# Up projection's last four chunks tile by tile, norm sums split between GpSimd and matmuls, factor diagonal on ScalarE

## What is computed

```python
def rmsnorm(x, g):
    y = x * lax.rsqrt(jnp.mean(x * x, axis=-1, keepdims=True) + EPS) * g
def sqrelu_mlp(h, w1, w2):
    return jnp.square(jax.nn.relu(h @ w1)) @ w2      # w1 (1024, 4096), w2 (4096, 1024)
for i in range(2):
    h = rmsnorm(x, norm_mix[i])
    x = x + (diff_attention(h, ...) if i == 0 else multiscale_pool(h, ...))
    x = x + sqrelu_mlp(rmsnorm(x, norm_mlp[i]), mlp_w1[i], mlp_w2[i])
```

## Time and profile before

| what | us |
|---|---|
| median of 3 runs | 1052.71 (1051.85 to 1053.17) |
| the profiled execution, its own time | 1052.46 |
| span of its trace | 1050.7 |
| PE busy in the span | 989.1 (94%) |
| DVE busy | 874.3 (83%) |
| ACT busy | 479.6 (46%) |
| POOL busy | 429.0 (41%) |

### The profile page before, as it was taken

One profiled execution on the slowest core, in us unless ns is written; L12 is line 12 of the kernel. 1 busy time (PEld: TensorE's weight loads), 2 busy tenths in 40 slices (PEclk: granted clock), 3 DMA queues, 4 the chain that ended last, 5 costly groups with the idle time before them and its releaser, 6 DMA issues.

```text
span 1050.7 us, 12852 instructions
## 1 busy us (share of the span) xinstructions
PE 989.1 (94%) x4676; PEld 802.4 (76%) x4676; DVE 874.3 (83%) x1125; ACT 479.6 (46%) x735; POOL 429.0 (41%) x377
## 2 busy tenths in 40 slices
PE   6999998889899799999999999798999999999998
PEld 5877776667677588887887887696887888788887
DVE  5667889877946999999998897676988989989884
ACT  4525555677644534425435353364452442543420
POOL 5852678556447173473840300371403304124000
PEclk9999999999999999999999999989999999999999
DMA  6423211120232333332333233301323333233102
GB/s 240 146 42 100 61 41 58 63 81 1 62 99 80 100 100 102 99 106 95 108 93 107 74 106 115 120 2 42 119 87 113 100 101 103 98 100 100 61 20 80
DMA packets 52046, 92.74 MB, mean 88 GB/s; under 512 B 8848, under 2 KB 9872, under 8 KB 51984
## 3 DMA queue, kind: packets, MB, share of 16 engines
q1 hardware_dynamic: 45888, 91.24, 27.4%
q10 hardware_dynamic: 6096, 0.69, 0.5%
HBM read 89.82 MB, written 2.10 MB: 87 GB/s over the span
## 4 chain that ended last, share of the span: by engine, by line
PE 53%; DVE 27%; issue 8%; POOL 5%; ACT 4%; DMA 1%; ACTq 1%; DVEq 0%; SPq 0%; POOLq 0%
PE bank L1572 51%; DVE s_s_raw L1342 3%; DVE s_acc L1360 3%; DVE s_lbB_lo L1137 3%; ACT s_u_raw L994 2%; DVE s_w_lo L1117 2%; DVE s_nmax L1227 2%; DVE s_u_raw L1324 2%; POOL s_nsum L727 2%; PE bank L1630 1%; DVE s_u_lo L1348 1%; DVE s_lt_lo L1137 1%; DVE s_p L1249 1%; DVE s_a_lo L1348 1%; POOL s_o_r L702 1%
## 5 line engine op out<-in xcount | busy, mean ns | idle before, releaser
L1572 PE MATMUL bank<-s_hT_hi,s_w_hi 128*128 128x512 f32 x512 | 200.5, 392 | 0.0
L1572 PE MATMUL bank<-s_hT_hi,s_w_lo 128*128 128x512 f32 x512 | 199.4, 389 | 0.0
L1572 PE MATMUL bank<-s_hT_lo,s_w_hi 128*128 128x512 f32 x512 | 199.4, 389 | 0.0
L1117 DVE TENSOR_TENSOR s_w_lo<-s_raw,s_w_hi 128x1024 fp32r<-128x1024 f32 x96 | 165.9, 1744 | 14.3 <-ACT s_w_hi L816 7.9
L1572 PE MATMUL bank<-s_b_hi,s_u_hi 128*128 128x512 f32 x288 | 117.1, 407 | 14.2 <-DVE s_a_lo L1348 10.4
L753 POOL TENSOR_TENSOR s_lt<-s_lbB,s_lbB 128x1024 f32<-128x1024 f32 x14 | 35.0, 2498 | 222.9 <-PE bank L1572 222.9
L846 ACT ACTIVATE s_b_hi<-s_lbB 128x1024 fp32r<-128x1024 f32 x64 | 67.3, 1054 | 128.2 <-POOL s_lbB L753 84.5
L1572 PEld LDWEIGHTS bank<-s_hT_lo,s_w_hi 128*128 128x128 f32 x512 | 96.2, 188 | 20.2 <-issue 0.5
L1572 PEld LDWEIGHTS bank<-s_hT_hi,s_w_hi 128*128 128x128 f32 x512 | 96.2, 188 | 20.2 <-issue 0.5
L1572 PEld LDWEIGHTS bank<-s_hT_hi,s_w_lo 128*128 128x128 f32 x512 | 96.1, 188 | 20.0
L1360 DVE TENSOR_TENSOR s_acc<-s_acc,bank 128x512 f32<-128x512 f32 x168 | 107.5, 677 | 2.0 <-PE bank L1572 2.0
(11 more groups left out here) (195 smaller groups left out, 2186.8 us busy)
## 6 DMA issues: line engine op xcount, KB each, us to landing
s_raw<-in_mlp_w SPq DMA_DIRECT2D x64, 512.0 KB, 3.8
s_lbB<-in_mlp_w SPq DMA_DIRECT2D x64, 512.0 KB, 3.3
s_raw<-in_attn_w_qkv SPq DMA_DIRECT2D x24, 512.0 KB, 4.2
s_raw<-in_attn_w_o SPq DMA_DIRECT2D x8, 512.0 KB, 3.4
s_x_nat<-in_x SPq DMA_DIRECT2D x4, 512.0 KB, 8.5
s_x_again<-in_x SPq DMA_DIRECT2D x4, 512.0 KB, 5.2
out<-s_acc SPq DMA_DIRECT2D x8, 256.0 KB, 2.0
s_raw<-in_pool_w SPq DMA_DIRECT2D x4, 256.0 KB, 2.6
```

The costliest lines, as they stand in the source:

```text
L1117: v.tensor_tensor(w_lo[slot][:, cols], raw[k][:], f32(w_hi[slot][:, cols]), ALU.subtract)\
L1572: return nc.tensor.matmul(o, lhsT, rhs, start=start, stop=stop, **kw)
```

## The change

The up phase takes the chunks 4 to 7 tile by tile instead of only 6 and 7. The sum of squares is divided: POOL adds the squares of chunks 0 to 5, and `stat` adds those of 6 and 7 by matmuls of their own, accumulated in the same place. The squares get four buffers instead of two, and the region moves to the accumulator of P7. In the first blocks `stat` comes after chunk 2. The factor diagonal is made by ACT in four tiles instead of by DVE in one. Orders on ACT and DVE are changed with it. The diff, cut where it only repeats:

```diff
+SUMMED = 6
...
-        nsum, nsq, diag = inside(v_region + P6 * 4 * 1024, ("nsum", [P, S], F32), ("nsq", [P, 2, S], F32),
+        nsum, nsq, diag = inside(v_region + P7 * 4 * 1024, ("nsum", [P, S], F32), ("nsq", [P, 4, S], F32),
...
 def norm_sums(m):                                    # POOL
-                for c in range(NC):
+                for c in range(SUMMED):
...
-                        pool.wait_ge(n_summed, (NC - 1) * m + c - 1)
-                    g.tensor_tensor(nsum[:], first_sum, nsq[:, c % 2, :], ALU.add).then_inc(n_summed, 1)
+                        pool.wait_ge(n_summed, (SUMMED - 1) * m + c - 1)
+                    g.tensor_tensor(nsum[:], first_sum, nsq[:, c % 4, :], ALU.add).then_inc(n_summed, 1)
...
 def w1_hi(b, k):                                     # ACT
-                if k < 3:
-                    act.wait_ge(up_piece, 3 * (b - 1) + k + 1)
+                if k < 2:
+                    act.wait_ge(up_piece, 2 * (b - 1) + k + 1)
                 else:
                     act.wait_ge(h1_ready, CH * b)
...
             def norm_tile(m, c):
+                norm_hi(m, c)
+                norm_square(m, c)
+            def norm_ready(m, c):
                 done, count = ((wo_added, NC), (xt_added, 0), (pool_added, 0))[m]
                 act.wait_ge(done, count + c + 1)
+            def norm_hi(m, c):
+                norm_ready(m, c)
                 a.activation(hT_hi[:, c, :], xT[:, c, :], ACT.Copy, scale=gcol[:, m, c:c + 1]).then_inc(n_hi, 1)
-                if m or c >= 2:
-                    act.wait_ge(n_summed, (NC - 1) * m + (max(1, c - 2) if c >= 2 else 0))
-                a.activation(nsq[:, c % 2, :], xT[:, c, :], ACT.Square).then_inc(n_squared, 1)
+            def norm_square(m, c):
+                norm_ready(m, c)
+                if c >= 4:
+                    act.wait_ge(n_summed, (SUMMED - 1) * m + max(1, c - 4))
+                elif m:
+                    act.wait_ge(n_stat, m)
+                a.activation(nsq[:, c % 4, :], xT[:, c, :], ACT.Square).then_inc(n_squared, 1)
...
+            def norm_diag(layer):
+                act.wait_ge(n_r, 2 * layer + 1)
+                for t in range(NT):
+                    a.activation(diag[:, t * P:(t + 1) * P], ident[:], ACT.Copy, scale=st_r[:, t:t + 1]).then_inc(n_diag, 1)
             def up_phase(b):                         # ACT
-                w2_hi(b, T3)
-                w1_hi(b + 1, 0)
-                w2_hi(b, T2)
-                w1_hi(b + 1, 1)
                 if first(b):
+                    if b:
+                        w2_hi(b, T3)
+                        w2_hi(b, T2)
+                        w1_hi(b + 1, 0)
+                    norm_diag(b // NB)
+                    if b == 0:
+                        w1_hi(b + 1, 0)
+                        w2_hi(b, T3)
+                    w1_hi(b + 1, 1)
                     spread_copy(b // NB)
+                else:
+                    w2_hi(b, T3)
+                    w1_hi(b + 1, 0)
+                    w2_hi(b, T2)
+                    w1_hi(b + 1, 1)
                 square(b, 0)
                 square(b, 1)
                 part_hi(b, A11)
                 part_hi(b, S3)
+                if b == 0:
+                    w2_hi(b, T2)
                 square(b, 2)
                 square(b, 3)
...
-            for c in range(NC):
+            for c in range(4):
                 norm_tile(1, c)
+            for c in range(4, NC):
+                norm_square(1, c)
+            for c in range(4, NC):
+                norm_hi(1, c)
...
             def up_phase(b):                         # DVE; its norm_diag is gone
                 if first(b):
...
                     w2_low(b, B11)
                     if b:
                         w2_low(b, T3)
-                        norm_diag(m)
                         w2_low(b, T1)
+                        w2_low(b, T2)
                         w1_lo(b + 1, 0)
-                        w2_low(b, T2)
                     else:
-                        norm_diag(m)
                         w1_lo(b + 1, 0)
+                        w2_low(b, T3)
                     w1_lo(b + 1, 1)
                     dve.wait_ge(n_rbc, b // NB + 1)
+                    hidden(b, 0)
                 else:
...
                     w2_low(b, T2)
+                    hidden(b, 0)
                     w1_lo(b + 1, 1)
-                hidden(b, 0)
                 hidden(b, 1)
                 part_sum(b, S3)
                 part_lo(b, A11)
-                hidden(b, 2)
-                if b == 0:
-                    w2_low(b, T3)
-                hidden(b, 3)
-                part_lo(b, S3)
                 if b == 0:
                     w2_low(b, T1)
+                hidden(b, 2)
+                part_lo(b, S3)
+                hidden(b, 3)
+                if b == 0:
                     w2_low(b, T2)
...
             for c in range(4, NC):
                 add_turned(c)
-                if c > 4:
-                    norm_lo(1, c - 1)
-            norm_lo(1, NC - 1)
+            for c in range(4, NC):
+                norm_lo(1, c)
...
             def up_last(b, f):                       # PE
-                if f == 0:
-                    pe.wait_ge(w_lo_done, 4 * w1_slab(b) + 4)
-                up_part(b, f, NC - 2)
-                up_part(b, f, NC - 1).then_inc(h1_ready, 1)
+                for c in range(4, NC):
+                    if f == 0 and c % 2 == 0:
+                        pe.wait_ge(w_lo_done, 4 * w1_slab(b) + c // 2 + 1)
+                    last = up_part(b, f, c)
+                last.then_inc(h1_ready, 1)
             def up(b):
-                for k in range(3):
+                for k in range(2):
...
             def stat(m):
-                pe.wait_ge(n_summed, (NC - 1) * (m + 1))
+                pe.wait_ge(n_squared, NC * (m + 1))
+                pe.wait_ge(n_summed, (SUMMED - 1) * (m + 1))
                 for t in range(NT):
-                    last = mm(bank[(7 + 4 * ((m + 1) // 2)) % 8][:, t:t + 1], nsum[:, t * P:(t + 1) * P], ones[:, 0:1], start=True, stop=True)
+                    dst, cols = bank[(7 + 4 * ((m + 1) // 2)) % 8][:, t:t + 1], slice(t * P, (t + 1) * P)
+                    mm(dst, nsum[:, cols], ones[:, 0:1], start=True)
+                    for c in range(SUMMED, NC):
+                        last = mm(dst, nsq[:, c % 4, cols], ones[:, 0:1], stop=c == NC - 1)
                 last.then_inc(n_stat, 1)
             def spread(n):
-                pe.wait_ge(n_diag, n + 1)
+                pe.wait_ge(n_diag, NT * (n + 1))
...
-            first_tiles(0, range(5))
+            first_tiles(0, range(3))
             stat(0)
-            first_tiles(0, (5,))
+            first_tiles(0, (3,))
             first_last(0)
...
-            first_tiles(NB, range(2, 6))
+            first_tiles(NB, (2,))
             stat(2)
+            first_tiles(NB, (3,))
             first_last(NB)
```

More of the change, by code:

```diff
@@ L1314, in norm_v @@
                     .then_inc(n_v, 1)
-            def norm_diag(m):
-                dve.wait_ge(n_r, m + 1)
-                v.tensor_tensor(diag[:].rearrange("p (t q) -> p t q", t=NT),
-                                ident[:].unsqueeze(1).to_broadcast([P, NT, P]),
-                                st_r[:, 0:NT].unsqueeze(2).to_broadcast([P, NT, P]), ALU.mult).then_inc(n_diag, 1)
             def hidden(b, f):
@@ L1365, in up_phase @@
                 if first(b):
-                    m = 2 * (b // NB)
-                    norm_v(m)
+                    norm_v(2 * (b // NB))
                     w2_low(b, B11)
@@ L1799, in first_last @@
             def first_last(b):
-                m = 2 * (b // NB)
-                pe.wait_ge(n_lo, NC * m + NC)
+                pe.wait_ge(n_lo, NC * 2 * (b // NB) + NC)
                 up_last(b, 0)
```

## The result

| us | before | after |
|---|---|---|
| median of 4 runs each | 1052.94 (1051.85 to 1059.13) | 1038.18 (1036.47 to 1039.57) |
| the profiled execution, span | 1052.46, 1050.7 | 1036.47, 1034.7 |

The ratio is 0.9847, 95% interval 0.9805 to 0.9889: 1.5% faster. The changed kernel, measured once more on another chip beside the kernel before, gave 1039.03 against 1052.71, ratio 0.9865 (0.9843 to 0.9887). The forecast of 1032.7 was 5.5 us too low; its range holds the result.

What follows compares the result with a forecast made beforehand. PE, busy 94% of the span, was taken to bound the kernel. Gains of 5.8, 5.2 and 9.0 made 20.0 us: 1052.46 to 1032.5, plus 0.25 for the median, 1032.7; range 1025.5 to 1040 for 8 in 10.

Steps and rivals of the forecast that it cites:

- the rival of the clock: The clock falls in the longer `stat`, in the first blocks and the pooling chain: 5 us lost, 1037.7; chance 0.2.
- that of the pooling: Pooling's gain is given back at DVE's locked low part and the additions behind: 4 to 6 us less, 1038; chance 0.1.
- the signs that I had named for being wrong: DVE ahead of PE at the end of up, `stat(0)` starting much after 324, or low clock following `stat`.
- Part 1: Chunks 4 to 7 tile by tile, hidden 0 earlier: A11's wait goes over 12 blocks, 5.8 us, bounds 4 and 9.7.
- The stop at the last product: At an ordinary block's last product, 0.39 us lost, expected to stay because POOL starts before DVE's low part of A22.
- the first rival: DVE starts before POOL at block end: last-product stop goes in some 10 blocks, 3.9 us more, 1028.8; chance 0.15.
- Hidden 0's place: In ordinary blocks, hidden 0 goes ahead of the last w1 split on DVE, so low A11 comes with over 1 us spare.
- Plain blocks: Blocks 7 and 15 were costed at nothing: DVE reaches hidden 0 late, or PE has turns of x between.
- Block 0: Products' 13th matmul starts at 345.8 against 351.02: 5.2 us gained, 1.2 of it low clock; bounds 3.7 and 6.7.
- `stat` (2.4 us): 24 matmuls instead of 8, 2.4 us instead of 0.80, adding 1.6 us of PE work in each of three places.
- Pooling and block 8: An earlier sum of squares and earlier windows, then block 8 without its stop: 9.0 us gained together, bounds 6 and 10.5.
- My bound for the lock: In the pooling, DVE's low part held behind POOL's last difference may move the 4.5 us gain between 3.2 and 5.8.

Runs made afterwards that it cites:

- experiment 6: Changed kernel with DVE taking low A22 before the P6 gathers and the P5 gathers before T4's low part; 1037.42 us, ratio 0.9812.
- experiment 8: Changed kernel with hidden 0 of ordinary blocks put back behind the last w1 split; 1036.27 us, ratio 0.982.
- experiment 7: Changed kernel with POOL's fourth difference of block 8 moved behind the norm's root; 1038.05 us, ratio 0.9833.
- the second execution: The profiled execution of the unedited changed kernel's repeated measurement on another chip; that measurement gave 1039.03 us, ratio 0.9865.
- experiment 10: Changed kernel with `stat` between chunk 3's matmuls in block 8 alone, and low A22 and P5 gathers moved earlier on DVE; 1033.88 us, ratio 0.9822.
- experiment 3: Changed kernel with `stat` placed between the matmuls of chunk 3 in blocks 0 and 8; 1036.86 us, ratio 0.983.
- experiment 9: Changed kernel with `stat` placed between the matmuls of chunk 3 in block 8 alone; 1037.13 us, ratio 0.9856.

## Why the prediction was right, and where it was off

*Faster, and the range:* right. The median lies at the rival of the clock (1037.7, chance 0.2) and at that of the pooling (1038, chance 0.1), not within the forecast's own 1029.5 to 1036. Of the signs that I had named for being wrong one came: the low clock follows `stat`. That the range holds the result is in part luck, since 2.0 us found elsewhere made up for some of what was missing: without them the median would be 1040.2, just outside.

*Part 1 (5.8 us):* right: the stop at the end of up is gone in all 14 blocks, 2.7 and 3.0 us over the two layers' ordinary blocks, alone 6.8 with the plain block. The stop at the last product stayed, as reckoned, for the reason given (experiment 6). My margin of 0.25 us in the first rival was real: in the changed kernel DVE comes 0.30 us behind POOL's start in block 9 (770.44, 770.14), and one gather of 0.6 us put behind the low part makes it 0.30 ahead (experiment 6). Hidden 0's place, of which I made a step, does nothing (experiment 8).

*Plain blocks (0):* wrong by 1.0 us. In block 7 the distance of starts ahead of the first down product fell from 1.34 to 0.36 us. In block 15 it stayed at 1.46.

*Block 0 (5.2 us):* the size is right, 5.8 and 4.2, its makeup isn't, so the size is luck. The matmul at 351.02, from which I reckoned, is the tenth of the products; the 13th starts at 351.70, so that my own steps give 5.9. Sum, diagonal and spread went as forecast: the 13th starts 29.69 us after the block, against 33.93. That is 4.2, less than 5.9 by 1.7, of which the low clock behind `stat` is 1.6. The other 1.5 came behind it, where I had S2's low part late by about 1 us again: with PE slower ahead of it that stop is gone, with full clock it is back with 0.69 (experiment 7), because DVE's splits behind POOL's differences are the next bound.

*`stat` (2.4 us):* 24 records took 2.6 to 2.7, 0.111 each, at full clock. The term was sized well. What I put apart as a rival, that the clock falls behind or in it, happened in five of the eight profiled executions that kept this row of 24 in block 0, 7 to 12 matmuls each time; behind `stat(2)` it cost 1.6, in four of the six that kept the row there, against my "up to 1.5 us in each first block".

*Pooling and block 8 (9.0 us):* this is the step that failed. Up to `stat(1)` it gave its 3.9. Behind it I had 5.1 more and got nothing. Three parts of it:
- "PE, which ran the pooling map in between at the low clock and now has the full one, starts the windows at 684.1", 6.4 us after `stat(1)`. It hasn't. PE stood 1.1 us ahead of `stat(1)`, and in all nine executions with that stop the clock still fell, 1.0 to 3.9 us after the row's start, in the row or in the map behind it; the windows start 7.0 to 8.8 us after `stat(1)`, against 6.93 before. I took the low clock of the map for a result of the stop of 5.3 us, and the stop's end for the clock's return. 0.5 to 2.3 us in the two executions. In the first, where DVE's fourth low part ends 6.7 us after the row's start, DVE's chain has a share in it.
- "From here the gain may shrink or grow by one lock": it shrank, from 1.86 to 2.60 us of the held low part, the stop grew from 0.69 to 1.44, and the clock fell behind it. Windows 2.5 to 3.6 us longer. My bound for the lock, 1.3 us, left the clock out. This is the largest part.
- The rest, 4.5 forecast from the last window to the end of block 8, was 4.1 where the clock held behind `stat(2)` and 2.5 where it didn't.

Of the 5.5 us between forecast and median, 3.4 is this sum (5.2 and 0.2 missing, 1.3, 0.6 and 0.1 found elsewhere), 0.5 is the stage ahead of block 0, and 1.5 that the profiled execution lay 1.7 below its median, where I had added 0.25. Where the clock falls explains a part of that: the second execution lost 2.8 us more in the same stages.

What stays open: what in the state of PE decides in which execution the clock falls behind the row; no run here controls it. That DVE's chain can hold up the squares of block 8 was seen in experiment 7 alone. Why the clock fell behind the stops of 0.91 us and more in the windows, and not behind those of 0.69 and less, is open too: no run set the length of that stop but experiment 7, which took it away. The 1.56 us of block 4 in experiment 6 came again with experiment 10 (that block 42.70 us); its cause, POOL's preparation of the band matrices beside DVE in that block alone, is read from the trace and wasn't tried.

## What to carry to other kernels

A short stop of PE is priced by what the clock does behind it as well, and a row of one-column matmuls in PE's stream can bring the same, even with PE busy by every row. Between wide matmuls they brought no fall in four places of experiments 3, 9 and 10, against nine falls behind the 14 rows of 24 that stood in the first blocks of the changed kernel and of those made from it; but where something waits for their sum this costs more than the fall (block 0 of experiment 3). Where two engines share a lock, the order on the one decides which of them waits, and a move that makes PE faster changes who comes first: look at each place where they meet, block by block. And compare stages by their length in the trace, not by the total, when a stage that isn't touched varies by more than the edit.

## What the runs showed that I had not expected

- Two executions of one program differ by 1.6 us in block 0 (46.43, 48.03) and by 1.8 us between `stat(1)` and the windows (6.97, 8.73), with the same stops to within 0.4 us and the clock falling at other places. The changed kernel's runs spread over 3 to 4.5 us; this, and the stage ahead of block 0 (317.8 to 324.1 in the profiled ones), are what the traces show for it.
- Four 128x128 copies with a factor on ACT take 1.28 us, 0.32 each; I had estimated 0.3.
- One-column matmuls of float32 follow each other after 0.111 us at full clock and 0.22 at the low level, half the time of one with 512 columns (0.227 and 0.43).
